# Reordering the TensorE work inside a routed expert job: both matrix products first, then both groups of transposes, with the gathered rows transposed two jobs ahead

## The reference, cut to what matters

```python
def moe_ffn(xf, ...):
    # router: sigmoid scores, best 4 of 8 groups, best 8 of 64 experts per token
    ...
    def expert_block(args):
        tok, e = args
        xb = x_pad[tok]
        return swiglu(xb, w_eg[e], w_eu[e], w_ed[e])   # silu(x@gate) * (x@up), then @down
    y = lax.map(expert_block, ...)                      # 64 experts, 1024 -> 256 -> 1024
    y = y * buf_w[:, None]
    routed = zeros.at[buf_tok].add(y)
    return routed + swiglu(xf, w_sg, w_su, w_sd)        # and one shared expert for every token
```

## Time and profile before

| | |
|---|---|
| median of 3 runs | 1691.76 us (1691.24 to 1693.01) |
| profiled execution, device time | 1691.86 us |
| span of its trace | 1690.1 us |
| mean granted clock of PE over the span | 0.95 |
| PE busy | 1560.7 us (92%) |
| DVE, ACT, POOL busy | 662.1, 293.5, 661.1 us |
| DMA | 319.36 MB, mean 189 GB/s |

### The profile page before, as it was taken

One profiled execution on the slowest core, in us unless ns is written; L12 is line 12 of the kernel. 1 busy time (PEld: TensorE's weight loads), 2 busy tenths in 40 slices (PEclk: granted clock), 3 DMA queues, 4 the chain that ended last, 5 costly groups with the idle time before them and its releaser, 6 DMA issues.

```text
span 1690.1 us, 24639 instructions
## 1 busy us (share of the span) xinstructions
PE 1560.7 (92%) x6759; PEld 691.5 (41%) x6760; DVE 662.1 (39%) x883; ACT 293.5 (17%) x573; POOL 661.1 (39%) x629
## 2 busy tenths in 40 slices
PE   7789898998897799899999999999999999999991
PEld 3455455554555444333333333333333333333330
DVE  1233432533434242344444444444444444444440
ACT  1223223223232100011111111111111111111110
POOL 2000202122022120156555555555555656565652
PEclk9799998898997799999999999999999999999995
DMA  9201111011116252479889988978889989888826
GB/s 354 75 21 44 43 27 44 15 41 44 24 44 249 56 133 87 190 233 302 287 269 321 310 294 261 300 219 256 252 264 337 343 259 311 281 265 254 293 45 114
DMA packets 71888, 319.36 MB, mean 189 GB/s; under 512 B 14791, under 2 KB 16328, under 8 KB 46388
## 3 DMA queue, kind: packets, MB, share of 16 engines
q1 hardware_dynamic: 41764, 237.52, 38.7%
q0 software_dynamic: 30096, 81.50, 21.1%
HBM read 279.59 MB, written 60.89 MB: 201 GB/s over the span
## 4 chain that ended last, share of the span: by engine, by line
PE 88%; DMA 3%; DVE 3%; issue 1%; POOL 1%; SPq 1%; ACT 1%; DVEq 0%; POOLq 0%; ACTq 0%
PE psP L626 50%; PE psW L626 28%; PE psT L763 5%; PE psW L793 2%; DMA area<-in_x_dram 1%; DMA u_dram<-zrow 1%; PE psW L672 1%; PE psT L632 1%; DVE area L1223 1%; PE psT L703 1%; DVE area L1119 1%; ACT area L904 0%; SPq L351 0%; PE psT L689 0%; SPq L347 0%
## 5 line engine op out<-in xcount | busy, mean ns | idle before, releaser
L626 PE MATMUL psP<-wts,area 128*64 (+2 forms) x2032 | 892.4, 594 | 21.1 <-DVE area L1119 11.8
L626 PE MATMUL psP<-area 128*64 128x512 f32 x1264 | 562.3, 598 | 0.0
L626 PEld LDWEIGHTS psP<-wts,area 128*64 128x64 f32 (+1 forms) x2032 | 317.6, 161 | 508.1 <-issue 499.2
L626 PE MATMUL psW<-wts,area 128*64 128x512 f32 (+2 forms) x1592 | 434.0, 601 | 4.0 <-DVE wts L1445 3.2
L587 POOL DMA_INDIRECT out_dram<-area,sidx x79 | 166.4, 2106 | 319.4 <-issue 164.0
L587 POOL DMA_INDIRECT x_dram<-area,sidx x79 | 244.9, 3100 | 24.1 <-issue 24.1
L626 PEld LDWEIGHTS psW<-wts,area 128*64 128x64 f32 (+1 forms) x1592 | 143.6, 148 | 221.1 <-issue 220.2
L1437 DVE COPY area<-wts 128x4096 f32 x81 | 185.8, 2294 | 97.5 <-issue 73.6
L1445 DVE COPY wts<-wts 128x2048 f32 x79 | 96.9, 1226 | 309.1 <-issue 309.1
L626 PEld LDWEIGHTS psP<-area 128*64 128x64 f32 x1264 | 167.3, 137 | 0.0
L1044 ACT ACTIVATE area<-psW 128x1024 f32<-128x1024 f32 x79 | 80.8, 1023 | 344.4 <-PE psW L626 253.6
(11 more groups left out here) (201 smaller groups left out, 828.3 us busy)
## 6 DMA issues: line engine op xcount, KB each, us to landing
wts<-in_w_exp_gate_dram SPq DMA_DIRECT2D x64, 1024.0 KB, 8.2
wts<-in_w_exp_up_dram SPq DMA_DIRECT2D x64, 1024.0 KB, 11.4
wts<-in_w_exp_down_dram SPq DMA_DIRECT2D x64, 1024.0 KB, 6.5
wts<-in_w_in_dram SPq DMA_DIRECT2D x4, 2048.0 KB, 17.7
area<-in_x_dram SPq DMA_DIRECT2D x8, 512.0 KB, 3.3
wts<-in_w_out_dram SPq DMA_DIRECT2D x1, 4096.0 KB, 18.3
area<-u_dram SPq DMA_DIRECT2D x16, 256.0 KB, 3.4
xn_dram<-area POOLq DMA_DIRECT2D x8, 512.0 KB, 3.0
```

Of the source, the lines that this page charges most:

```text
L626: return nc.tensor.matmul(out_, lhsT, rhs, start=start, stop=stop)
```

## The change: the diff

Order of PE within job j after: gate_up(j), down(j-1), t_job(j+2), t_h(j). `xT` becomes a list of two tensors, chosen by the parity of the job; the second lies in `bias`, which only the front uses. gather runs four jobs ahead of scatter where it ran three. At the seam from shared to routed jobs, DVE's copy_gu(1, 1) moves ahead of h_mul(NSH) and read_shared(NSH - 1), and SP's store of the last shared result moves behind the load of expert 3's weights. In the shared jobs the same order of PE is used; ahead of them one t_job more is done.

```diff
-        xT = cut(D).rearrange("p (k n) -> p k n", k=KT)
+        xT = [cut(D).rearrange("p (k n) -> p k n", k=KT),
+              bias[:, 0:NH // 2, :].rearrange("p h (a n) -> p (h a) n", n=P)]
...
-            shared_out(NSH - 1, (NSH - 1) % 2)
...
             load_w(0, w_exp_gate[0, 3], w_exp_up[0, 3], w_exp_down[0, 3])
+            shared_out(NSH - 1, (NSH - 1) % 2)
...
             gather(NSH + 2, 0, 2)
+            gather(NSH + 3, 1, 3)
...
-                    gather(j + 3, 1 - k, i * 6 + (3 + 3 * k))
-                    scatter(j, k, i * 6 + (4 + 3 * k))
+                    gather(j + 4, k, i * 6 + (4 + 3 * k))
+                    scatter(j, k, i * 6 + (5 + 3 * k))
...
             for j in range(1, NSH):
                 if j >= 2:
                     gate_up(j, j % 2)
-                if j + 1 < NSH:
-                    t_job(j + 1, (j + 1) % 2, r_ld, (j + 1) // 2 + 1)
                 else:
-                    t_job(NSH, 0, g_ld, 1)
+                    t_job(2, 0, r_ld, 2)
                 down(j - 1)
+                q = j + 2
+                if q < NSH:
+                    t_job(q, q % 2, r_ld, q // 2 + 1)
+                else:
+                    t_job(q, q % 2, g_ld, 1)
...
                     gate_up_halves(r + NSH, k, (now % NSLOT) * SLOTW)
-                    t_job(r + NSH + 1, 1 - k, g_ld, i + (1 + k))
                     down_halves(r + NSH - 1, (was % NSLOT) * SLOTW)
+                    t_job(r + NSH + 2, k, g_ld, i + 2)
                     t_h(r + NSH)
...
-            def read_xT(j):
+            def read_xT(j, par):
                 dve.wait_ge(s_xg_t, j + 1)
-                if not (isinstance(j, int) and j == 0):
-                    dve.wait_ge(s_gu, j)
-                V.tensor_copy(xT, psT[:, :, :]).then_inc(s_xT_ready, 1)
+                if not (isinstance(j, int) and j < 2):
+                    dve.wait_ge(s_gu, j - 1)
+                V.tensor_copy(xT[par], psT[:, :, :]).then_inc(s_xT_ready, 1)
...
             for j in range(1, NSH):
                 h_mul(j, j % 2, one_col[:, 0:1])
-                read_xT(j + 1)
+                if j == 1:
+                    read_xT(2, 0)
                 read_shared(j - 1, (j - 1) % 2)
+                read_xT(j + 2, j % 2)
...
             dve.wait_ge(s_tab, 3)
+            copy_gu(1, 1)
             h_mul(NSH, 0, tab_w[:, 0:1])
             read_shared(NSH - 1, (NSH - 1) % 2)
-            copy_gu(1, 1)
-            read_xT(NSH + 1)
+            read_xT(NSH + 2, 0)
             copy_dn(0)
             copy_gu(2, 0)
             h_mul(NSH + 1, 1, tab_w[:, 1:2])
-            read_xT(NSH + 2)
+            read_xT(NSH + 3, 1)
...
                     h_mul(r + NSH, k, tab_w[:, bass.ds(r, 1)])
-                    read_xT(r + (NSH + 1))
+                    read_xT(r + (NSH + 2), k)
                     copy_dn(r)
                     copy_gu(r + 2, k)
```

More of the change, by code:

```diff
@@ L604, in jobs @@
                     j = i * 2 + (NSH + k)
-                    gather(j + 3, 1 - k, i * 6 + (3 + 3 * k))
-                    scatter(j, k, i * 6 + (4 + 3 * k))
+                    gather(j + 4, k, i * 6 + (4 + 3 * k))
+                    scatter(j, k, i * 6 + (5 + 3 * k))
             routed_jobs(pool, 0, jobs)
-            pool.wait_ge(g_ld[0], ((n + 4) // 2) * 16)
-            pool.wait_ge(g_ld[1], ((n + 3) // 2) * 16)
+            pool.wait_ge(g_ld[0], ((n + 5) // 2) * 16)
+            pool.wait_ge(g_ld[1], ((n + 4) // 2) * 16)
             for b in range(2):
@@ L772, in gate_up @@
                 for k in ks:
-                    i = mm(psP[:, par, :].rearrange("p (m f) -> p m f", m=2), xT[:, k, :], w[:, :, k, :], k == 0,
+                    i = mm(psP[:, par, :].rearrange("p (m f) -> p m f", m=2), xT[par][:, k, :], w[:, :, k, :], k == 0,
                            k == KT - 1)
@@ L783, in gate_up_halves @@
                 for k in range(KT):
-                    mm(psP[0:HB, par, :].rearrange("p (m f) -> p m f", m=2), xT[:, k, 0:HB], w[:, :, k, :], k == 0,
+                    mm(psP[0:HB, par, :].rearrange("p (m f) -> p m f", m=2), xT[par][:, k, 0:HB], w[:, :, k, :], k == 0,
                        k == KT - 1)
-                    i = mm(psP[HB:P, par, :].rearrange("p (m f) -> p m f", m=2), xT[:, k, HB:P], gu_b[par][:, :, k, :],
+                    i = mm(psP[HB:P, par, :].rearrange("p (m f) -> p m f", m=2), xT[par][:, k, HB:P], gu_b[par][:, :, k, :],
                            k == 0, k == KT - 1)
@@ L1358, in _ @@
             dve.wait_ge(s_xn_st, 16 * NT)
-            read_xT(0)
+            read_xT(0, 0)
             route(TL)
             read_pos(TL)
-            read_xT(1)
+            read_xT(1, 1)
             slots(TL)
```

## The result

| | before | changed |
|---|---|---|
| median, 4 runs each | 1692.38 us | 1667.62 us (1665.19 to 1668.51) |
| ratio | | 0.985, 95% interval 0.9833 to 0.9867 |
| span of the profiled execution | 1690.1 us | 1666.0 us |

The time fell by 24.8 us, where 32 were forecast. It lies inside the range of 1655 to 1684 and above the forecast's own 1656 to 1664.

The account below looks back on a forecast made before the run. PE, busy in every window of the routed stage, was taken as the bound. Seams -23.5, stage stall -8.6, extra t_job +0.9 and end -0.8 made -32.0 us from 1691.86: 1659.9, predicted as 1660, range 1655 to 1684.

Parts of the forecast that it names:

- The seams of a job: PE, routed jobs: two changes of tile instead of four save 0.298 us per job, 23.5 us over 79 jobs.
- a gate_up of 7.02: Sign of being wrong, PE's routed jobs: gate_up still 7.02 us before down, where 6.87 was expected.
- DVE, ACT and weights at no cost: Routed jobs: DVE's moved copies, ACT's earlier read_y and the weight loads make PE wait no longer, 0 us.
- the rival of late weights: Routed stage: shorter jobs make weight loads the bound, returning part of the 23.5 us, 1665 to 1680 us; chance 0.06.
- The stall at the seam of the stages: Second routed job: PE's 5.66 us stall and the 2.91 us of lower clock behind it both vanish, 8.57 us.
- The store behind the weights: SP's last shared store lands between 710 and 712, holding gather(12) on POOL; stall 0 to 1.7 us, taken as 0.
- the second rival: Early stall: t_job(12) waits for the gather behind the late store, then lower clock, 1662 to 1667 us; chance 0.10.
- If a gather shows among PE's releasers: Sign of being wrong: the profile after the change shows PE waiting for a gather.
- One t_job more and the start: PE ahead of the jobs: one more t_job, +0.87 us; lost hiding of register reads, 0 to +0.3, taken as 0.
- The end: Last job: last down ends at 20.5, plus 2.3 gives 22.8, later than POOL's 22.4; today 23.6, so -0.8 us.
- the rival in which the seams keep their price: Routed jobs: 0.149 belongs to every change of product, 1683.4 us, or 1672 if one seam keeps it; chance 0.14 together.
- The rival of the instruction stream: Head of each routed job: PE's register reads show, up to 1.0 us per job, 79 us, 1739 us; chance 0.08.

Follow-up runs that it names:

- experiments 1 and 2: Changed kernel with t_job back between gate_up and down (four changes of tile): 1694.02 us; with t_job in two parts around half of down (six): 1716.4 us.
- experiment 3: Changed kernel with both groups of transposes done as products with the identity in pairs of 128*64 tiles, so no change of tile: 1817.74 us.
- experiment 5: Kernel before with only DVE's order at the seam changed, copy_gu(1, 1) ahead of h_mul(8) and read_xT(9) ahead of read_shared(7): 1685.23 us, ratio 0.9951.
- Experiments 6 and 7: Changed kernel with the last shared store ahead of expert 3's weights again: 1663.07 us; with the store left there but awaited only by the scatters: 1663.2 us.
- best: Changed kernel with the last shared store ahead of expert 3's weights and DVE's copy_dn ahead of read_xT in the routed loop: 1660.32 us, ratio 0.9808.
- order_single: Kernel before with only the new PE order in the routed jobs, one xT and x one job ahead: 1778.75 us.

## Why the prediction was right, and where it was off

**The seams of a job**, the largest term: right in mechanism and size. 0.298 us per job were forecast, 0.30 measured; experiments 1 and 2 show that they follow the number of changes of tile and nothing else of the change. Two things beside the tile are ruled out: register addresses by down's 3.43, since the seam gate_up|down has them and costs nothing, and the step between products and transposes by the shared jobs, where it costs nothing at 128\*128, and by experiment 3 at the seam from down. At t_h|gate_up experiment 3 can't tell.

Where the price shows was forecast wrongly: the prediction listed 6.87 + 3.59 + 0.87 + 0.37, the price in the piece ahead of a change of tile, and took a gate_up of 7.02 for a sign of being wrong. The runs show 7.02 + 3.43 + 1.02 + 0.22, the price in the piece behind the change. The total is the same, and the trace before, with 0.15 on all four pieces, could not tell the two apart; the sign was badly chosen.

The Trainium skill ("TensorEngine Tiling (Array Packing)", Key Properties) says that changing the tiling mode drains the engine. The runs show a price for each change, 0.149 us; that it is a drain they don't show. The Trainium skill's rule weighed in the prediction ("TensorE: Matmul & The Clock Gate", Part 3), that a load overlaps matmuls only in another row group, does not hold at this seam: the load came 0.43 us ahead. The same section also lets a load into the background weight buffer go ahead, which the prediction left out.

**DVE, ACT and weights at no cost**: right. The timeline of DVE in the changed kernel, for a job that starts at 1188.0 (against the earlier trace rows):

```profile
1202.04 1.23 DVE L1450 COPY wts<-wts 128x2048 f32 x1 [1.22 <-issue]
...
1204.45 2.29 DVE L1442 COPY area<-wts 128x4096 f32 x1 [1.18 <-issue]
...
1207.38 0.68 DVE L1355 SCALAR_TENSOR_TENSOR kv_sb<-kv_sb,area,psP 128x256 f32<-128x256 f32 x1 [0.63 <-ACT kv_sb L1033]
```

copy_dn starts 14.0 into its job and copy_gu 16.4, both as worked out, and the next h_mul waits for ACT's silu, not for DVE. From 800 to 1600 us DVE waits for a weight load 6 times, where it did 18 times before, so the rival of late weights is absent. From t_h to t_h every routed job behind the first but the two around the new wait is within 0.03 us of 11.69.

**The stall at the seam of the stages**, 8.57 us: right, and shown alone by experiment 5 (8.3 us by the runs, 8.53 in the trace).

**The store behind the weights** is the step that failed: "stall 0 to 1.7 us. I take 0." It cost 6.49: a wait of 3.92 and 2.57 of lower clock behind it, for which the term held nothing. The store landed at 714.5, 13.6 us after the first of the weights was issued, where 9 to 11 had been counted (710 to 712 from 701). The sum let 3.7 MB pass at 434 GB/s, the highest rate of the old burst. By the windows, 4.6 MB moved from 700.97 to 714.53, at 337 GB/s on average. So 0.9 MB more than the weights ahead and the store themselves went first. SP issues the next expert's 2 MB only 2.2 us behind the store; that these are the 0.9 MB is argued from the order of issues, not tested. POOL then took 3.9 us from the landing to the gather, its register reads among them; the prediction's 714.5 for the gather's issue, for which it shows no working, lies 3.5 behind the middle of its landing times. PE was ready 1.0 us later than forecast. That left 5.8 us for a gather instead of 8.8, and it took 9.65, within the 10.5 that the prediction had as its bound. This mechanism was the second rival, with 1662 to 1667 us; the measured 1667.6 lies just above it. "If a gather shows among PE's releasers" was one of the prediction's signs of being wrong, and rightly so. Experiments 6 and 7 confirm it by taking it out in two ways.

**One t_job more and the start**: +1.80 where 0.87 was taken. The t_job itself is 0.88. 0.73 is there before the first difference in order (the second shared gate_up starts at 604.40, not 603.67), so it comes from the front, which the change doesn't touch. 0.17 is less cover for the register reads at the first routed job (1.11 instead of 0.94).

**The end**: -0.8 was forecast, +0.67 - 1.09 = -0.4 measured. copy_dn started 14.4 in the last job, not 14.0, and the last wait became 4.2 us. The later of the two chains was named rightly (the last down, not POOL).

**The number**: the four terms missed by 0.1, 6.5, 0.9 and 0.4 us, all to the same side, 7.9 together. That the time still lies in the range is in part luck: the forecast's own range, 1656 to 1664, misses it, and the range reached up to 1684 for the rival in which the seams keep their price, which is false. The rival that came true had been named, with a chance of 0.10.

**The rival of the instruction stream**: absent from the changed kernel, whose "issue" waits at line 628 are one of 1.1 us. Experiment 3 has gaps that fit it, with many short matmuls as the last things ahead of the register reads, but no run shows that they come from there.

## What to carry to other kernels

When the bounding engine shows no waits, add up its pieces against the same pieces in another stage: 0.15 us at every seam was invisible in busy time and in the waits, and the half of the seams that could be spared was 1.4% of the kernel. Put work of one tile form together, and look for what must be doubled so that the new order has no copy in its way. When a transfer is moved past others in a queue, follow it to whoever waits for its landing, and to what is queued behind that wait; here a store nobody reads held up a gather.

## What the runs showed of the hardware that was not expected

POOL's small copy of indices, at most 0.71 us in every job of the kernel before, takes 2.4 to 2.8 us in nearly all jobs after the change. The timeline of the changed kernel, POOL and DVE:

```profile
1215.76 2.81 POOL L571 COPY gidx<-area 128x1 int32 x1
1216.25 2.29 DVE L1442 COPY area<-wts 128x4096 f32 x1 [1.29 <-issue]
```

Both end at 1218.55, though the copy of 128 elements started first. From 800 to 1600 us 67 of the 68 index copies are long, and 64 of these end within 0.06 us of the end of a copy_gu on DVE. In the kernel before none of the 67 lies beside a copy_gu, and none is long. So the time of this small POOL instruction depends on what DVE does beside it. It costs nothing here, since POOL has room.

A PE wait of 3.9 us was followed by the lower granted clock, and so were the 3.2 us ahead of the last down of the kernel before and 2.4 us in best (the last down of best took 5.37 us where it takes 3.43 at full clock; the granted clock of the window from 1618 to 1620 us is 0.50). The 1.4 us waits in every job of order_single were not: its granted clock is 1.00 from 800 to 1600 us.

At the head of each job in experiment 3, PE stands still for 0.4 to 1.1 us, where the changed kernel shows nothing of the kind behind its first routed job. The Trainium skill ("TensorE: Matmul & The Clock Gate", Wait — 56ns, not 53.3ns?) gives about 62 ns of sequencer time per matmul where the decoding is done in microcode. By that figure the 32 matmuls of t_job in experiment 3 would take at least 1.98 us (an estimate). They took 1.75 us, 55 ns each, close to the 1.71 expected from streaming, so this cost is not what bounds them here. What makes the gap stays open.
